# One core, hybrid attention encoder with experts: probabilities copied inside the on-chip memory by SyncE's queue and turned as float32r, big transfers moved to GpSimd's queue

## What is computed

```python
def block_attention(q, k, v, scale):            # q (S, 8 heads, D), k and v (S, heads, D)
    sc = einsum(q, k) * scale
    p = softmax(sc, axis=-1)
    return einsum(p, v)

def encoder_layer(x, p):
    proj = rms_norm(x) @ w_in
    oa = block_attention(qa, ka, va, 64 ** -0.5)     # 8 query heads on 2 key/value heads, width 64
    ob = block_attention(qm, km, vb, 96 ** -0.5)     # 8 heads from low-rank latents, width 96, values 64
    x = x + concat(rms_norm(oa), rms_norm(ob)) @ w_o
    h2 = rms_norm(x)
    return x + expert_choice_moe(h2)                 # 16 experts, each takes its 64 best tokens, SwiGLU of width 1024
```

## Time and profile before

| | us |
|---|---|
| median of 3 runs | 1082.65 (1082.18 to 1087.85) |
| the profiled execution's own time | 1086.1 |
| its span, first to last instruction | 1083.7 |
| PE busy | 1044.8 (96%) |
| DVE busy | 886.0 (82%) |
| ACT busy | 775.3 (72%) |
| POOL busy | 423.3 (39%) |

### The profile page before, as it was taken

The page is one execution under the profiler, slowest core; times in us unless marked ns, Lnnn a source line. Parts: engine busy times, 40 slices in busy tenths (PEclk is TensorE's granted clock), DMA queues, the critical chain, the costliest instruction groups (busy, mean ns, idle before and its releaser), DMA issues.

```text
span 1083.7 us, 16970 instructions
## 1 busy us (share of the span) xinstructions
PE 1044.8 (96%) x5689; PEld 896.7 (83%) x5689; DVE 886.0 (82%) x1147; ACT 775.3 (72%) x1095; POOL 423.3 (39%) x394
## 2 busy tenths in 40 slices
PE   8999999999999999998699999999999999999995
PEld 7999978999889987887578888888888888888884
DVE  6787669989999843338899999999999999999991
ACT  7655569888998843344577877877878878788771
POOL 2466576111358502334524432344323444234101
PEclk9999999999999999999799999999999999999998
DMA  8232050010211348741799999999999999999982
GB/s 305 79 116 102 1 197 1 2 41 20 98 41 40 98 109 263 225 164 79 235 417 378 398 400 400 400 421 400 401 400 400 413 408 401 400 400 406 415 310 39
DMA packets 77936, 266.05 MB, mean 245 GB/s; under 512 B 11249, under 2 KB 13516, under 8 KB 77628
## 3 DMA queue, kind: packets, MB, share of 16 engines
q1 hardware_dynamic: 69776, 239.68, 56.9%
q0 software_dynamic: 8048, 25.68, 8.3%
q10 hardware_dynamic: 60, 0.01, 0.0%
HBM read 239.07 MB, written 26.28 MB: 245 GB/s over the span
## 4 chain that ended last, share of the span: by engine, by line
PE 48%; DVE 2%; DMA 1%; issue 1%; ACT 0%; POOLq 0%; POOL 0%; DVEq 0%; ACTq 0%
PE ps L2003 10%; PE ps L2005 10%; PE ps L2004 10%; PE ps L2017 5%; PE ps L2019 5%; PE ps L2018 5%; PE ps L1980 1%; DMA xe<-h,idxT 1%; DMA out<-y,give 1%; DVE lo L2171 0%; DVE idx L1776 0%; DVE affT L1785 0%; DVE gates L1771 0%; ACT hi L2093 0%; POOLq L2274 0%
## 5 line engine op out<-in xcount | busy, mean ns | idle before, releaser
L2171 DVE TENSOR_TENSOR lo<-raw,hi 128x2048 fp32r<-128x2048 f32 x191 | 430.0, 2285 | 32.3 <-ACT hi L2093 32.0
L2093 ACT ACTIVATE hi<-raw 128x2048 fp32r<-128x2048 f32 x192 | 364.6, 1918 | 70.0 <-PE ps L2005 57.3
L2003 PE MATMUL ps<-hi,xehi 128*128 128x512 f32 x480 | 188.3, 392 | 1.3 <-DVE h L2193 1.0
L2005 PE MATMUL ps<-hi,xelo 128*128 128x512 f32 x480 | 186.9, 389 | 0.0
L2004 PE MATMUL ps<-lo,xehi 128*128 128x512 f32 x480 | 186.8, 389 | 0.0
L1939 POOL DMA_INDIRECT xe<-h,take x60 | 111.1, 1851 | 25.1 <-issue 13.7
L2003 PEld LDWEIGHTS ps<-hi,xehi 128*128 128x128 f32 x480 | 90.1, 188 | 20.2 <-issue 1.4
L2005 PEld LDWEIGHTS ps<-hi,xelo 128*128 128x128 f32 x480 | 90.1, 188 | 18.8
L2004 PEld LDWEIGHTS ps<-lo,xehi 128*128 128x128 f32 x480 | 90.2, 188 | 18.1
L1934 POOL COPY take<-idx 128x4 uint32 (+1 forms) x15 | 29.0, 1930 | 193.7 <-DVE xt L2187 187.4
L1361 DVE TENSOR_TENSOR probTlo<-ps,probThi 128x512 fp32r<-128x512 f32 x128 | 87.8, 686 | 12.1 <-ACT probThi L1318 10.0
(11 more groups left out here) (302 smaller groups left out, 2192.3 us busy)
## 6 DMA issues: line engine op xcount, KB each, us to landing
raw<-in_w_down SPq DMA_DIRECT2D x64, 1024.0 KB, 10.0
raw<-in_w_gate SPq DMA_DIRECT2D x60, 1024.0 KB, 9.7
raw<-in_w_up SPq DMA_DIRECT2D x60, 1024.0 KB, 9.3
w_raw<-in_w_in SPq DMA_DIRECT2D x8, 592.0 KB, 9.0
x<-in_x SPq DMA_DIRECT2D x8, 512.0 KB, 3.7
woraw<-in_w_o SPq DMA_DIRECT2D x4, 1024.0 KB, 5.1
o<-attention_out SPq DMA_DIRECT2D x8, 512.0 KB, 4.4
xr<-in_x SPq DMA_DIRECT2D x8, 512.0 KB, 7.0
```

Of the source, the lines that this page charges most:

```text
L2003: pe.matmul(ps[:, dst[n], :], rowhi[:, c, :], hi[w][:, cols], start=c == 0, stop=False)
L2005: last = pe.matmul(ps[:, dst[n], :], rowlo[:, c, :], hi[w][:, cols], start=False, stop=c == KD - 1)
L2093: act.activation(hi[s][:], raw[s][:], ACT.Copy).then_inc(hi_done, 1)
L2171: dve.tensor_tensor(lo[s][:], raw[s][:], hi[s][:].bitcast(F32), ALU.subtract).then_inc(lo_done, 1)
```

## The change

- The identity matrix is written as float32r.
- For units 0 to 5 nothing changes. From unit 6 on, SP waits for the exponential of unit `v`, and for the turn of unit `v - 3`, and copies the 128x512 float32 probabilities (256 KB) from `att["p"][v % 3]` to one of three new buffers `turn`, all in the on-chip memory. PE turns from there and waits for the landing where it had waited for the exponential; ACT's next exponential into the same buffer waits for the landing where it had waited for the turn. The phases keep their index (there is no additional step).
- A turned unit is read, and written to the accumulator memory, as float32r, except where `u` is a multiple of 4, which stays float32. Those are the units whose turns alternate with a head's output.
- At even `u`, where there is a values product, the four turns no longer stand ahead of it. Each stands ahead of one of the four low-part matmuls L1215.
- The stores of the heads and the loads of the output weights are issued by POOL, at the key heads named in `stores`. `route_first` is cut to the attended rows of tile 0 and issued in the middle of SP's copies (at unit 94), and the residual of tile 0 goes to `route_second`. SP's list goes on to `route_second` and `route_rest` after its last copy. The store of the last group of heads is POOL's, ahead of its routing work.
- Three buffers (`wr`, `o0` and the new ones) are placed elsewhere.

```diff
@@ project, gpsimd_program
-        pool.affine_select(out=k["ident"][:], in_=k["ident"][:], compare_op=ALU.not_equal, fill=1.0,
+        pool.affine_select(out=k["ident"][:].bitcast(F32R), in_=k["ident"][:], compare_op=ALU.not_equal, fill=1.0,
@@ attend
+    turn = att["turn"]
+    turn_loaded = project_signals["w_loaded"][0:len(turn)]
+    DIRECT = 6
+    def loaded(v):
+        return turn_loaded[v % 3], 16 * (v // 3)
+    def exp_read(v):
+        return (pt_ready, v + 1) if v < DIRECT else loaded(v)
...
+    def store_heads(engine, s, h0, h1):
+        cols = slice(h0 * VD, h1 * VD)
+        engine.wait_ge(o_done, HEADS * s + h1)
+        engine.dma_start(o_rows[TS * s:TS * (s + 1), :, cols].rearrange("t p d -> p t d"),
+                         att["rows"][s][0][:, :, cols]).then_inc(o_stored, 16)
@@ sync_program
-        for h0, h1 in O_PARTS:
-            store_heads(0, h0, h1)
-        sp.wait_ge(o_stored, 16 * len(O_PARTS))
-        for i in range(KD // 2):
-            if i >= 2:
-                sp.wait_ge(wo_lo, 2 * (i - 1))
-            sp.dma_start(wo["raw"][:, 2 * (i % 2):2 * (i % 2) + 2, :],
-                         a["w_o"].rearrange("(k p) n -> p k n", p=P)[:, 2 * i:2 * i + 2, :]).then_inc(wo_loaded, 16)
-        route_first(sp)
-        for h0, h1 in O_PARTS[:-1]:
-            store_heads(1, h0, h1)
+        for v in range(DIRECT, NU):
+            sp.wait_ge(exp_done, v + 1)
+            sp.wait_ge(pt_ready, v - 2)
+            sp.dma_start(turn[v % 3][:], att["p"][v % 3][:]).then_inc(turn_loaded[v % 3], 16)
+            if v == NU // 2 + 30:
+                route_first(sp)
         route_second(sp)
-        store_heads(1, *O_PARTS[-1])
         route_rest(sp)
@@ gpsimd_program
+        stores = {QH + 5: (0, 0), HEADS: (0, 1), HEADS + GROUP: (0, 2), HEADS + QH + 4: (1, 0), HEADS + QH + 6: (1, 1)}
...
+            if g in stores:
+                s, part = stores[g]
+                store_heads(pool, s, *O_PARTS[part])
+                if (s, part) == (0, len(O_PARTS) - 1):
+                    pool.wait_ge(o_stored, 16 * len(O_PARTS))
+                    load_output_weights(0)
+                    load_output_weights(1)
             for i in split_after.get(g, ()):
                 split_output_weights(pool, i)
+                if i in (1, 3):
+                    load_output_weights((i + 3) // 2)
+        store_heads(pool, SETS - 1, *O_PARTS[-1])
@@ tensor_program
             if i == 0:
-                pe.wait_ge(exp_done, u + 1)
+                if u < DIRECT:
+                    pe.wait_ge(exp_done, u + 1)
+                else:
+                    pe.wait_ge(*loaded(u))
...
-            turned = pe.transpose(ps[:, T_BANKS[u % 2], cols], att["p"][u % 3][:, cols], k["ident"][:])
+            rows = att["p"] if u < DIRECT else turn
+            as_type = F32 if u < DIRECT or u % TS == 0 else F32R
+            turned = pe.transpose(ps[:, T_BANKS[u % 2], cols].bitcast(as_type), rows[u % 3][:, cols].bitcast(as_type),
+                                  k["ident"][:].bitcast(as_type))
...
                 else:
+                    if between is not None:
+                        transpose_prob(between, i)
                     pe.matmul(ps[0:VD, OT_BANK, cols], v[:, i, 0, :], ptlo[m % 2][:, i, :], start=False, stop=False)
...
-            for i in range(TS):
-                if output is not None:
-                    turn_output(output, i)
-                if turned is not None:
-                    transpose_prob(turned, i)
             if pair is not None:
-                values(pair)
+                values(pair, turned)
+            else:
+                for i in range(TS):
+                    if output is not None:
+                        turn_output(output, i)
+                    if turned is not None:
+                        transpose_prob(turned, i)
@@ scalar_program
                 if v >= 3:
-                    act.wait_ge(pt_ready, v - 2)
+                    act.wait_ge(*exp_read(v - 3))
@@ route
     def sync_first(sp):
+        sp.wait_ge(o_stored, 16 * len(O_PARTS))
+        load_attended(sp, 0)
+
+    def sync_second(sp):
         sp.wait_ge(wo_lo, KD)
-        load_rows(sp, 0)
+        load_residual(sp, 0)
         sp.wait_ge(score_ready, UNITS)
         load_rows(sp, 1)
```

More of the change, by code:

```diff
@@ L252, in build @@
         att["ot"] = bm("ot", [P, SEQ])
+        att["turn"] = [bm("turn0", [P, SEQ])]
         assert bm.at <= w_in_end, (bm.at, w_in_end)
@@ L262, in build @@
         wo["small"] = om("smallo", [P, 128])
-        wo["wr"] = om("wr", [P, KD, EXPERTS])
         wo["aff"] = [om(f"aff{i}", [P, 64]) for i in range(2)]
+        att["turn"] += [om(f"turn{i}", [P, SEQ]) for i in (1, 2)]
         assert om.at <= end
         om3 = Map(temps_at)
-        wo["o"], wo["x"] = [om2("o0", [P, D])], [om2("xr0", [P, D])]
+        om2.at += D * 4
+        wo["x"] = [om2("xr0", [P, D])]
         wo["othi"], wo["otlo"] = [om2("othi0", [P, KD, P], F32R)], [om2("otlo0", [P, KD, P], F32R)]
@@ L274, in build @@
         assert om2.at <= w_in_end
+        wo["o"] = [None]
         for i in (1, 2):
@@ L280, in build @@
         wo["gffn"] = om3("gffn", [P, D])
+        wo["wr"] = om3("wr", [P, KD, EXPERTS])
+        wo["o"][0] = om3("o0", [P, D])
         assert om3.at <= weights_at, (om3.at - weights_at)
@@ L970, in project @@
     signals = {"rows_ready": rows_ready, "mla_ready": mla_ready, "kv_done": kv_done, "proj_done": proj_done,
-               "row_copied": row_copied, "halves_ready": halves_ready, "rows_set": rows_set, "pj_back": pj_back, "mla_back": mla_back, "xlo_done": xlo_done, "clo_done": clo_done}
+               "row_copied": row_copied, "halves_ready": halves_ready, "rows_set": rows_set, "pj_back": pj_back, "mla_back": mla_back, "xlo_done": xlo_done, "clo_done": clo_done,
+               "w_loaded": w_loaded}
     return (sync_program, gpsimd_program, tensor_program, scalar_program, vector_program), signals
@@ L1112, in split_output_weights, with load_output_weights @@
             pool.tensor_tensor(wo["lo"][:, i, :], raw, wo["hi"][:, i, :].bitcast(F32), ALU.subtract).then_inc(wo_lo, 1)
+        def load_output_weights(i):
+            if i >= 2:
+                pool.wait_ge(wo_lo, 2 * (i - 1))
+            pool.dma_start(wo["raw"][:, 2 * (i % 2):2 * (i % 2) + 2, :],
+                           a["w_o"].rearrange("(k p) n -> p k n", p=P)[:, 2 * i:2 * i + 2, :]).then_inc(wo_loaded, 16)
+        stores = {QH + 5: (0, 0), HEADS: (0, 1), HEADS + GROUP: (0, 2), HEADS + QH + 4: (1, 0), HEADS + QH + 6: (1, 1)}
         split_after = {HEADS + GROUP: (0, 1), HEADS + QH: (2, 3), HEADS + QH + 1: (4,), HEADS + QH + 2: (5,),
@@ L1193, in transpose_prob, with values @@
             cols = slice(i * P, (i + 1) * P)
-            turned = pe.transpose(ps[:, T_BANKS[u % 2], cols], att["p"][u % 3][:, cols], k["ident"][:])
+            rows = att["p"] if u < DIRECT else turn
+            as_type = F32 if u < DIRECT or u % TS == 0 else F32R
+            turned = pe.transpose(ps[:, T_BANKS[u % 2], cols].bitcast(as_type), rows[u % 3][:, cols].bitcast(as_type),
+                                  k["ident"][:].bitcast(as_type))
             if i == TS - 1:
                 turned.then_inc(pt_ready, 1)
-        def values(m):
+        def values(m, between):
             g, qi = units[2 * m]
@@ L1450, in route, with load_attended, load_residual @@
     at_ready, at_done, merged, psteps, vsteps = sem("at_ready"), sem("at_done"), sem("merged"), sem("pool_steps_r"), sem("vector_steps_r")
+    def load_attended(sp, j):
+        sp.dma_start(o[j % 3][:], o_rows[ORDER[j]]).then_inc(o_loaded[j % 3], 16)
+    def load_residual(sp, j):
+        sp.dma_start(xr[j % 3][:], x_dram[ORDER[j]]).then_inc(xr_loaded[j % 3], 16)
     def load_rows(sp, j):
-        sp.dma_start(o[j % 3][:], o_rows[ORDER[j]]).then_inc(o_loaded[j % 3], 16)
-        sp.dma_start(xr[j % 3][:], x_dram[ORDER[j]]).then_inc(xr_loaded[j % 3], 16)
+        load_attended(sp, j)
+        load_residual(sp, j)
     def sync_first(sp):
+        sp.wait_ge(o_stored, 16 * len(O_PARTS))
+        load_attended(sp, 0)
+    def sync_second(sp):
         sp.wait_ge(wo_lo, KD)
-        load_rows(sp, 0)
-    def sync_second(sp):
+        load_residual(sp, 0)
         sp.wait_ge(score_ready, UNITS)
```

5 lines of the change are left out of this document (removed).

## The result

| us | before | after |
|---|---|---|
| median of 4 runs each | 1083.58 (1082.18 to 1087.85) | 1109.16 (1107.42 to 1111.66) |
| ratio, 95% interval | | 1.0234 (1.0216 to 1.0252) |
| span of the profiled execution | 1083.7 | 1108.1 |
| attention, first to last exponential | 231.9 | 261.4 |
| last exponential to the end of the routing's last merge | 139.5 | 136.7 |

The kernel is slower by 2.3%, where 1% faster was forecast. The three stretches say where: the attention is 29.5 us longer, what lies behind it 5.3 us shorter. Of these 5.3, the 2.5 of the last stretch need not be the change's, since the profiled execution of before (1086.1) lies 2.5 us above the median of the four runs here and the one after (1110.47) only 1.3. So I read the attention first.

What follows compares the result with a forecast made beforehand. PE was taken to bound the attention, DVE next. Gains of 3.2 (grouped-query) and 6.1 (latent), less 0.5 (sharing) and 0.6 (last copy), plus 2.5 (end), made 10.7 us: 1082.65 to 1072, range 1068 to 1077.

Steps and rivals of the forecast that it cites:

- float32r turns: PE's turns in the attention: 0.43 us less per head; net gains 3.2 us in grouped-query heads, 6.1 in latent heads.
- copy on the path: Between exponential and turn: landings exceed the shortest gaps, costing 0.18 us per grouped-query head, nearly nothing in latent heads.
- big transfers beside the copies: Six stores and four weight loads share the rings, making the next one or two copies late: 0.5 us in all.
- end of attention, lists of SP and POOL: After the last exponential: the copy costs 0.6 us; earlier issue of tile 2's rows gains 2.5 us.
- C = 1.9: Copy between exponential and turn: 1.9 us for 256 KB including semaphores, extrapolated from larger stores; bounds 1.5 and 2.8.
- The closed loop: Exponential, copy, turn, high part, next exponential: four jumps cover three heads, 10.0 + 4C; 5.87 us per head forecast.
- A bare turn: PE's turns in units 2 modulo 4: the weight load binds at 0.11 us, so float32r gains 0.
- rival 2: PE's weight loads stay cheap for float32r turns: 0.21 us more per head, total gain 16, 1066.5 us; chance 0.17.
- A pair: PE's turn plus low-part matmul in odd units: from 0.223 to 0.17 us, 0.43 us less per head.
- rival 4: DVE and longer turns take up PE's gain: grouped-query heads gain 0, latent 0.25 each; 1077 us, chance 0.14.
- DVE's floor of 6.28: Grouped-query heads: least time per head DVE allows, 6.57 less its 0.29 us idle.
- Rival 1: The copy's loop binds with landings nearer 2.8 us: 7.07 us per grouped-query head, kernel at 1089; chance 0.15.

Runs made afterwards that it cites:

- exp. 3: Changed kernel without copies; ACT writes the probabilities rounded to float32r, and three units of four are turned as float32r: 1074.61 us, ratio 0.9898.
- exp. 4: Changed kernel with its copies, but the transfers POOL issues in between made small (output differs): 1090.25 us, ratio 1.0052.
- experiment 1: Changed kernel with no copies: all units turned in float32 straight from the exponential's buffers, the rest of the change kept: 1081.53 us, ratio 0.9971.
- experiment 9: Changed kernel with turns and later phases one index later, a fourth turn buffer, and big transfers on SP's queue in 256 KB pieces: 1088.05 us, ratio 1.0035.
- experiment 13: Changed kernel with turns and later phases one index later, a fourth turn buffer, and head stores and output-weight loads cut small (output differs): 1075.7 us, ratio 0.9935.

## Why the prediction was wrong

The sum, term by term, in us:

| term | forecast | measured |
|---|---|---|
| float32r turns | -9.3 (3.2 grouped-query, 6.1 latent) | about -7: 0.34 per latent head, next to nothing per grouped-query head (exp. 3) |
| copy on the path, no big transfer beside it | in the 3.2, 0.18 per head | +15.3 (exp. 4 less exp. 3) |
| big transfers beside the copies | +0.5 | +20.8 (exp. 4) |
| end of attention, lists of SP and POOL | -1.9 | -2.8 from last exponential to merge; -3.1 in the whole time of experiment 1 |

- **The copy's C = 1.9 was the first step that failed.** C is the time from the end of the exponential's sum to the copy's landing. It was extrapolated from 384 and 512 KB to 256 KB. Measured: a landing after 2.2 to 2.3 us, and 2.28 or more from sum to turn. The size hardly counted: 256 KB took what the 384 KB of the earlier trace rows had taken; the line through two rows was a choice near the favourable end. By the forecast's own count of gaps, 2.3 + 0.05 instead of 1.95 leaves 0.86 missing in unit 17, 0.61 in the next, and about 0.4 in each of the other five under 2.0 us: 3.5 us in four heads, 0.88 each, and 6.57 - 0.43 + 0.88 = 7.0. Measured: 6.83. That it comes so near is in part luck: the 0.43 was not there to be had (6.54 per head in experiment 3), and from 6.54 the count gives 7.4, too much. Its direction was right, and it turned on 0.4 us of C. The closed loop, (10.0 + 4 x 2.3) / 3 = 6.4, is no guide: it leaves out where on the way each gap lies. Latent heads, "nearly nothing" in the forecast, are up too, 8.15 against 7.88: their 1.91 is also under 2.3, and two of the copies there (issued at 211.4 and 227.3) take 3.2 and 3.3 us. The forecast gave every quiet copy one and the same C; most of experiment 4's waits (8.8 of 14.8 us) are for the eleven that took more than 3.0, for which the sum has no term.
- **"I charge 0.5 us in all" for the sharing with stores and loads failed by a factor of 40.** The forecast priced a late copy as late by itself. But at one load three copies land 6.6 to 8.4 us after their issue, the phases have no slack for it, and all engines stop; the half clock comes on top, which the forecast knew from the earlier trace rows and did not apply here. That a transfer beside others is late by several us stood in the trace before, for a store issued at 367.8 us with three more in flight, against the 2.8 of the earlier trace rows:

```profile
attention_out<-pj SPq DMA_DIRECT2D x1, 512.0 KB, 7.6
```

- **The turn was mis-sized both ways.** A bare turn went to 0.064 us, not 0.11: the weight load stayed cheap (141 ns as in the earlier trace rows), as rival 2 had it. A pair went to 0.18, not 0.17. In the grouped-query heads neither counts, 26.14 against 26.26 us for four heads, as in rival 4; but DVE's floor of 6.28 wasn't reached, and PE waits there for DVE's results while DVE itself has idle time (experiment 3). Rival 2's own sum has 3.5 us for the end where the forecast's terms give 2.5, without a reason.
- **Right:** the end. No wait on tile 2's rows, no half clock behind them, rows issued 2.7 us sooner after the last turn of the probabilities (429.66 - 415.72 against 401.52 - 384.90), POOL's list without a wait on values.
- **Rival 1** had the mechanism, a copy that binds, and 1089 for it. Experiment 4 measures 1090.25 when the transfers are cut down. That it is so near is luck again: rival 1 wanted C near 2.8, and the quiet copies land after 2.2 to 2.3, under the 2.43 from which its loop would bind. The other 20 us no rival had.

What remains open: why the four loads still hurt copies on the same queue in pieces of 256 KB (experiment 9), and what the packets of q8 cost, which no run took away.

## What to carry to other kernels

A copy put between a producer and its consumer costs its whole landing time (2.2 us at least here for 256 KB, and 2.3 before for 384 KB), so compare it, and its late cases (3.1 to 3.9 us with no big transfer beside it), with the shortest gaps in the loop, and buy slack with an additional step: where no big transfer was near, that alone brought PE back to full. A small transfer on which every engine waits must not run beside large ones. Price the sharing as a stall of the whole pipeline, clock included, and try first what needs no copy, here ACT's write as float32r, if its rounding can be borne.

## What was not expected of the hardware

- The turn of 128x128 float32r took 0.064 us from start to start, with the float32 turn at 0.11; its weight load is shown at 141 ns in both.
- A load of 1 MB from DRAM, issued by POOL, landed after 8.8 us beside the copies, and three of them landed after 6.6 to 8.4 us instead of 2.3; for 2.5 us only the load's queue moved packets. With transfers cut down the longest copy took 3.9.
- All eleven copies over 3.0 us in experiment 4, and all twelve in experiment 13, had a packet of 16 KB of the queue q8, instruction, under way.
- After TensorE had stood still for 5.4 us, its granted clock was 0.50 to 0.62 for more than 4 us of work.
